# Head pairs of an RWKV layer: three levels of a triangular inverse as a loop on TensorE, and two products moved to GpSimd

## The reference

```python
def wkv_scan(r, decay, k, v, a_vec, b_vec, s0, reverse):
    def step(s, inp):
        r_t, w_t, k_t, v_t, a_t, b_t = inp
        sa = jnp.einsum('bhvk,bhk->bhv', s, a_t)
        s = s * w_t[:, :, None, :] + sa[..., None] * b_t[:, :, None, :] + v_t[..., None] * k_t[:, :, None, :]
        return s, jnp.einsum('bhvk,bhk->bhv', s, r_t)
    xs = tuple(jnp.swapaxes(t, 0, 1) for t in (r, decay, k, v, a_vec, b_vec))
    s_final, ys = lax.scan(step, s0, xs, reverse=reverse)
    return jnp.swapaxes(ys, 0, 1), s_final
...
for d in range(N_DIRS):
    yc_d, s_ctx = wkv_scan(r_c, dec_c, k_c, vh_c, -kk_c, kk_c * a_c, s0, reverse)
    yx_d, _ = wkv_scan(r_x, dec_x, k_x, vh_x, -kk_x, kk_x * a_x, s_ctx, reverse)
```

## Time and profile before

| | us |
|---|---|
| median of three runs | 4356.76 |
| lowest and highest | 4350.53, 4363.58 |
| the profiled execution | 4341.01 |
| its span from first to last instruction | 4339.2 |
| mean granted TensorE clock | 0.963 |

### The profile page before, as it was taken

The page is one execution under the profiler, slowest core; times in us unless marked ns, Lnnn a source line. Parts: engine busy times, 40 slices in busy tenths (PEclk is TensorE's granted clock), DMA queues, the critical chain, the costliest instruction groups (busy, mean ns, idle before and its releaser), DMA issues.

```text
span 4339.2 us, 93368 instructions
## 1 busy us (share of the span) xinstructions
PE 3897.5 (90%) x39960; PEld 2507.8 (58%) x39960; DVE 1669.7 (38%) x3445; ACT 852.2 (20%) x1847; POOL 663.0 (15%) x643
## 2 busy tenths in 40 slices
PE   5989999989967777777889998999999989999998
PEld 4534444445456766766444444447688854658887
DVE  2512122154545445445232112453345424515363
ACT  2200000020154444444100001115000011330000
POOL 4100000000022222222000000000334310003343
PEclk8989999999989999999899999999999999999999
DMA  8387887851200000000369996110122221102221
GB/s 334 142 307 293 333 333 293 335 218 72 81 8 13 13 13 13 13 13 17 136 264 428 429 429 277 59 59 1 65 91 78 78 86 39 40 20 78 93 82 39
DMA packets 54242, 619.74 MB, mean 143 GB/s; under 512 B 5648, under 2 KB 8976, under 8 KB 18320
## 3 DMA queue, kind: packets, MB, share of 16 engines
q1 hardware_dynamic: 49664, 599.41, 35.0%
q10 hardware_dynamic: 2448, 9.05, 0.6%
q0 software_dynamic: 1792, 6.29, 0.5%
HBM read 602.40 MB, written 12.32 MB: 142 GB/s over the span
## 4 chain that ended last, share of the span: by engine, by line
issue 44%; PE 42%; DMA 4%; DVE 3%; POOLq 3%; POOL 2%; ACT 1%; DVEq 0%; PEld 0%; SPq 0%; ACTq 0%; PEldq 0%
PE bank L891 29%; PE bank L1362 12%; DMA ring<-slabs 3%; POOL work L3257 1%; POOLq L3260 1%; POOLq L3258 1%; DMA kv<-work 1%; POOLq L3174 1%; POOL work L3261 1%; PE bank L1409 1%; DVE work L2699 0%; DVE work L2379 0%; PEld bank L891 0%; ACT work L2084 0%; DVE work L2723 0%
## 5 line engine op out<-in xcount | busy, mean ns | idle before, releaser
L891 PE MATMUL bank<-ring,work 128*32 128x256 f32 (+3 forms) x7002 | 765.6, 440 | 71.0 <-DMA ring<-slabs 59.1
L891 PE MATMUL bank<-work 128*128 128x256 f32 (+8 forms) x3590 | 785.8, 430 | 26.1 <-DVE work L3100 15.9
L891 PEld LDWEIGHTS bank<-work 128*128 128x128 f32 (+3 forms) x3590 | 500.5, 184 | 298.2 <-issue 212.7
L891 PEld LDWEIGHTS bank<-ring,work 128*32 128x32 f32 (+2 forms) x7002 | 317.9, 124 | 493.5 <-issue 387.2
L891 PE MATMUL bank<-work,ring 128*128 128x256 f32 (+1 forms) x1616 | 480.7, 456 | 12.1 <-DVE work L3119 5.1
L891 PE MATMUL bank<-hx,ring 128*128 128x512 f32 (+1 forms) x1344 | 482.8, 515 | 6.6 <-DVE hx L2394 4.5
L1362 PE MATMUL bank<-work 64*64 64x64 f32 x11520 | 338.5, 233 | 123.8 <-issue 87.2
L891 PEld LDWEIGHTS bank<-work,ring 128*128 128x128 f32 x1616 | 306.6, 191 | 181.2 <-issue 134.2
L1362 PEld LDWEIGHTS bank<-work 64*64 64x64 f32 x11520 | 309.6, 144 | 162.0 <-issue 158.1
L891 PEld LDWEIGHTS bank<-hx,ring 128*128 128x128 f32 x1344 | 256.7, 192 | 220.5 <-issue 200.2
L3177 POOL TENSOR_TENSOR work<-work 128x512 f32<-128x512 f32 (+1 forms) x30 | 34.4, 1156 | 1458.1 <-ACT work L1913 1458.1
(11 more groups left out here) (317 smaller groups left out, 4587.2 us busy)
## 6 DMA issues: line engine op xcount, KB each, us to landing
ring<-slabs SPq DMA_DIRECT2D x228, 2048.0 KB, 10.0
work<-slabs SPq DMA_DIRECT2D x48, 2048.0 KB, 18.3
work<-kv SPq DMA_DIRECT2D x18, 384.0 KB, 3.2
kv<-work SPq DMA_DIRECT2D x2, 3072.0 KB, 15.7
kv<-work ACTq DMA_DIRECT2D x6, 512.0 KB, 17.6
work<-tabs ACTq DMA_DIRECT2D x1, 2176.0 KB, 8.2
resx<-xT SPq DMA_DIRECT2D x1, 2048.0 KB, 10.9
outT<-hx ACTq DMA_DIRECT2D x8, 256.0 KB, 2.1
```

Source lines behind the costliest of these rows:

```text
L891: return pe.matmul(out, lhsT, rhs, start=(k == 0), stop=(k == n - 1))
```

## The change

Levels 2, 3 and 4 become a loop of three turns on TensorE alone; the other engines stay written out. A loop's waits need numbers that grow by the same amount each turn, so the steps of levels leave the common orders and get semaphores of their own: `lv_dve` for T additions, `lv_act` for copies, `lv_pool` for masks, with orders `LV_DVE`, `LV_ACT` and `LV_POOL`. The chain steps leave levels 2 to 4: four (d = 0) or five (d = 1) come between the values' products, three stay in level 1, four (d = 0) or three (d = 1) stand in level 5. Gate and bonus products come after level 5. The sums of the key norm, the variance and the gate use other banks. `decayed_bs` and `decayed_keys` run on GpSimd, after the masks of level 4 and of level 5. The core of the diff:

```diff
+LV_DVE, LV_ACT, LV_POOL = [], [], []
+EARLY = (4, 5)
...
+    RK_PE += [("x0", _d, 0), ("pre", _a, 0), ("pre", _a, 1), ("x0", _d, 1), ("x0", _d, 2)] + _zs(1)
+    RK_PE += [("mv", _d, 0)] + _zs(1) + [("mv", _d, 1)] + _zs(1) + [("mv", _d, 2)] + _zs(1)
+    RK_PE += [("kn", 0)] * _d + _zs(_d) + [("kn", 1), ("var",)] * _d
     for _l in range(1, 6):
...
+        _n = _l in (1, 5)
+        RK_PE += [("T", _d, _l, 0), ("T", _d, _l, 1)] + _zs(_n) + [("T", _d, _l, 2), ("XX", _d, _l, 0)] + _zs(_n)
+        RK_PE += [("XX", _d, _l, 1)] + _zs(_l == 5) + [("XX", _d, _l, 2)] + _zs(_n)
+    RK_PE += [("gate",), ("bonus",)] * _d
...
-RK_BANK = {"vt": (0, 1), "x0": (2, 3, 2), "mv": (0, 1, 0), "kn": (4, 5), "var": (7,), "T": (2, 3, 2), "gate": (7,), "bonus": (6,), "mean": (6,),
+RK_BANK = {"vt": (0, 1), "x0": (2, 3, 2), "mv": (0, 1, 0), "kn": (1, 4), "var": (5,), "T": (2, 3, 2), "gate": (5,), "bonus": (6,), "mean": (6,),
...
+            def level_products(d, l, b):
+
+                out = P[RK_BANK["T"][b]]
                 for q, c in enumerate(chunks(b)):
                     m = heads2(out[:, q * CH:(q + 1) * CH], NL[:, c, :], X[:, c, :], across=l > 1)
-                m.then_inc(rk_pe, rk.one("T", d, l, b))
+                return m
...
+            def middle_levels(p, d):
+
+                nl, xx, ts = (lv_count(order, p, (name, d, 2, 0)) for order, name in ((LV_POOL, "nl"), (LV_ACT, "XX"), (LV_DVE, "T")))
+                with pe.Fori(0, 3) as i:
+                    for b in range(3):
+                        pe.wait_ge(lv_pool, i * 3 + (nl + b))
+                        pe.wait_ge(lv_act, i * 3 + (xx - 3 + b))
+                        if b == 2:
+                            pe.wait_ge(lv_dve, i * 3 + ts)
+                        pe.sem_inc(pe_steps)
+                        level_products(d, 2, b).then_inc(rk_pe, 1)
+                    for b in range(3):
+                        pe.wait_ge(lv_dve, i * 3 + (ts + b))
+                        if b == 2:
+                            pe.wait_ge(lv_act, i * 3 + xx)
+                        pe.sem_inc(pe_steps)
+                        double_products(d, 2, b).then_inc(rk_pe, 1)
...
             def scores(p, d, b):
...
-                outb, = banks(p, "sb", d, b, after=[("dve", 0, "kds", d)])
+                outb, = banks(p, "sb", d, b, after=[("pool", 0, "kds", d), ("dve", 0, "arr", d)])
...
                     first_levels(p, d, 1, 2)
-                    values_in(p, d)
+                    chain(p, a, 1)
+                    values_in(p, d, 0)
+                    chain(p, a, 2)
+                    values_in(p, d, 1)
+                    chain(p, a, 3)
+                    values_in(p, d, 2)
+                    chain(p, a, 4)
                     if d == 1:
-                        key_sums(p)
+                        key_sums(p, 0)
+                        chain(p, a, 5)
+                        key_sums(p, 1)
                         head_sums(p, "var", sqs, "act", ("sq",))
...
+                    j = EARLY[d]
+                    level_t(p, d, 1, 0)
+                    level_t(p, d, 1, 1)
+                    chain(p, a, j + 1)
+                    level_t(p, d, 1, 2)
+                    level_x(p, d, 1, 0)
+                    chain(p, a, j + 2)
+                    level_x(p, d, 1, 1)
+                    level_x(p, d, 1, 2)
+                    chain(p, a, j + 3)
+                    middle_levels(p, d)
+                    level_t(p, d, 5, 0)
+                    level_t(p, d, 5, 1)
+                    chain(p, a, j + 4)
+                    level_t(p, d, 5, 2)
+                    level_x(p, d, 5, 0)
+                    chain(p, a, j + 5)
+                    level_x(p, d, 5, 1)
+                    chain(p, a, j + 6)
+                    level_x(p, d, 5, 2)
+                    if d == 0:
+                        chain(p, a, j + 7)
+                    else:
+                        gate_product(p)
+                        head_sums(p, "bonus", ksr, "dve", ("ksr",))
...
-                act.wait_ge(*(rk_done("dve", p, "pp") if d == 0 else rk_done("dve", p - 1, "kds", 0)))
+                act.wait_ge(*(rk_done("dve", p, "pp") if d == 0 else rk_done("pool", p - 1, "kds", 0)))
...
-            def decayed_bs(p, d):
-
-                v.wait_ge(*rk_done("dve", p, "ksm", d))
-                v.tensor_tensor(bd, bd, E3, ALU.mult).then_inc(rk_dve, rk.next("bds", d))
...
+            def decayed_bs(p, d):
+
+                pool.wait_ge(*rk_done("dve", p, "ksm", d))
+                pool.wait_ge(*rk_done("act", p, "exps", d))
+                pool.tensor_tensor(bd, bd, E3, ALU.mult).then_inc(rk_pool, rk.next("bds", d))
+
+            def decayed_keys(p, d):
+
+                pool.tensor_tensor(kd, kd, E3, ALU.mult).then_inc(rk_pool, rk.next("kds", d))
...
+                        if l == 4:
+                            decayed_bs(p, 1 - d)
+                        elif l == 5:
+                            decayed_keys(p, 1 - d)
```

More of the change, by code:

```diff
@@ L161 @@
         _by = {"sb": ("act", ("nt",) + _rest), "sk": ("dve", ("mt",) + _rest), "mean": ("dve", ("cen",)), "gate": ("dve", ("res",))}
[L162 removed]
+        _by.update({_q: ("dve", _name) for _q in ("x0", "ar", "bonus")}, T=("lvd", _name))
         RK_READ[_name] = {RK_BANK[_k][_rest[-1] if _rest else 0]: [_by.get(_k, ("act", _name))]}
@@ L1372, in banks @@
                 freed = [(engine, before) + step for steps in RK_FREE[name].values() for engine, step, before in steps
-                         if not (front and (step[0] in ("bonus", "res", "XX") or engine == "act" and step in RK_ACT[:RK_ACT.index(("pw", 0))])) and not (back and step[0] != "z")]
+                         if not (front and (step[0] in ("bonus", "res", "mv") or engine == "act" and step in RK_ACT[:RK_ACT.index(("pw", 0))])) and not (back and step[0] != "z")]
                 for engine in ("dve", "act", "pool"):
@@ L1378, in banks @@
                         pe.wait_ge(*rk_done(engine, p + last[0], *order[last[1] - 1]))
+                for engine, order in (("lvd", LV_DVE), ("lva", LV_ACT), ("lvp", LV_POOL)):
+                    last = max(((-step[1], place_in(order, step[2:])) for step in list(after) + freed if step[0] == engine), default=None)
+                    if last and p + last[0] >= 0:
+                        pe.wait_ge(*lv_done(engine, p + last[0], *order[last[1] - 1]))
                 pe.sem_inc(pe_steps)
@@ L1388, in first_levels @@
                 for b in groups:
-                    out, = banks(p, "x0", d, b, after=[("pool", 0, "nl", d, 0, b)])
+                    out, = banks(p, "x0", d, b, after=[("lvp", 0, "nl", d, 0, b)])
                     for q, c in enumerate(chunks(b)):
@@ L1486, in inverse_times @@
             def inverse_times(p, d, b):
-                out, = banks(p, "wu", d, b, after=[("act", 0, "XX", d, 5, b), ("act", 0, "mv", d, b)])
+                out, = banks(p, "wu", d, b, after=[("lva", 0, "XX", d, 5, b), ("act", 0, "mv", d, b)])
                 for q, c in enumerate(chunks(b)):
@@ L2853, in _ @@
                     first_levels(p, d)
-                    steps = iter(range(1, NCH))
+                    for j in range(1, EARLY[d] + 1):
+                        chain(p, a, j)
+                    steps = iter(range(EARLY[d] + 1, NCH))
                     for l in range(1, 6):
@@ L2857, in _ @@
                         level(p, d, l, 1)
-                        for j in itertools.islice(steps, 1):
-                            chain(p, a, j)
+                        if l in (1, 5):
+                            chain(p, a, next(steps))
                         level(p, d, l, 2)
-                        for j in itertools.islice(steps, 1):
-                            chain(p, a, j)
+                        if l in (1, 5):
+                            chain(p, a, next(steps))
                         if l == 1:
@@ L2868, in _ @@
                             decayed_sums(p, a)
-                        elif l == 4:
-                            decayed_bs(p, a)
-                        for j in itertools.islice(steps, 1):
-                            chain(p, a, j)
+                        if l in (1, 5):
+                            chain(p, a, next(steps))
+                        if l == 5 and d == 0:
+                            chain(p, a, next(steps))
                         if l == 1 and d == 1:
```

112 lines of the change are left out of this document (51 added, 61 removed).

## The result

| | before | after |
|---|---|---|
| median (runs) | 4354.55 us (4) | 4320.44 us (4) |
| lowest and highest | 4350.53, 4363.58 | 4310.69, 4327.15 |
| the profiled execution | 4341.01 | 4327.15 |
| the stage, first addition of x0 (cut 0.2 us ahead of it) to last state copy | 1223.1 to 2075.1, 852.0 | 1238.7 to 2058.8, 820.1 |

The ratio is 0.9917, 95% interval 0.9894 to 0.9939: faster by 34 us. Forecast was 4334 (23 us less), with 4312 to 4344 for the likeliest case alone. The stage of the profiles doesn't hang on that. The stage got 31.9 us shorter where the sum said 24.

A forecast was written before the change was run, and what follows sets the result against it. TensorE, standing for its own code packets, was taken as the bound; loop, chain steps, decays and the rest summed to -1.4 us even, -1.6 odd, -23 in all, giving 4334 us; range leaving out two in ten 4292 to 4375.

The forecast's parts named there:

- the likeliest case: Whole kernel: the change takes it to 4334 us, own range 4312 to 4344; chance 0.45 for -13 to -45 us.
- the sum: Pass over the head pairs: -1.4 us an even and -1.6 an odd half-pass, eight pairs -24, with the prologue -23.
- The bound: Pass over the head pairs: TensorE's code comes one packet at a time, 4 us each; it stands about 1 us a packet.
- The loop: Levels 2 to 4 on TensorE: 14.5 us as a loop, saving 3.2 us an even and 3.0 an odd half-pass.
- The chain steps: Early part, levels 1 and 5: moved steps make TensorE work and stand there, +2.6 us even, +1.7 odd half-pass.
- The decays: Inverse-decay products moved from VectorE to GpSimd: -0.5 us an even half-pass, 0 odd, +1 before the loop over p.
- More comes back: Half-passes: chain's waits hide in code waits, a level takes 3.9 us; about -4 us a half-pass, 4293 us; chance 0.13.
- A wash: Levels 2 to 4: a level takes 4.9 us and the chain takes the saving; 4344 to 4370 us; chance 0.20.
- the two slower ones for chain and GpSimd: Moved steps stand 0.54 us each: 4387 us, chance 0.15; level 5's masks late by 1.8 us: 4363 to 4375, 0.04.
- Branches that fetch: TensorE's loop: each taken branch takes 3.86 us, 124 us in all; about 4458 us; chance 0.03.

The follow-up runs named there:

- the small kernels: Two kernels of their own: 1728 plain matmuls, written out or looped 101.0 us each; matmuls in the level's order (64 columns), 96.8 us written out, 71.2 us looped.

## Why the prediction was right

**The bound.** Right, and now shown: 128 matmuls and a stop. Code came at 3.45 to 4.01 us a packet where I read 4.0 to 4.5, and a packet holds 256 records, not 249. In the small kernels the price of a packet is that time less the time TensorE needs for it, so nothing at 29.2 ns a matmul and about 1 us at 20.6.

**The loop.** 145 packets (140 to 150 forecast), "issue" -46 us (-25 to -50), branches of 212 ns, levels 2 to 4 in 14.0 and 13.1 us (14.5). The term was mis-sized: a level takes 3.83 us, not 4.2, so that 3.7 and 4.4 us a half-pass (without gate and bonus) were saved, for 3.2 and 3.0. Not all of it is the loop's: with the loop undone levels 2 to 4 take 15.4 and 15.1 us, so 2.3 and 2.4 us of it come from what left these levels. What the term left out is the gain behind the loop: with the loop undone, "rest" is 1.1 to 1.8 us longer, where the forecast had 0.3. That the fetch gets ahead during the loop would explain it; it fits the 0.8 to 1.0 us of "issue" there, but no row shows it.

**The chain steps.** The place was right, the form not. In the early part I expected waits of 1 to 2 us; the profile shows one of 0.4 a half-pass, and the part is still 1.4 and 1.2 us longer (1.9 and 1.4 were put there), since a step and the values' product beside it follow at the chain's pace of some 0.8 us. The waits forecast for level 5 don't exist in the profile: no row of the chain's update there. Together with what their absence saves in levels 2 to 4, chain steps, banks and decays lose 19 us of stage where there is no loop to gain by them.

**The decays.** 2.27 and 1.81 us on GpSimd for 1.8 twice; the masks of level 5 end no wait of TensorE. The forecast -0.5 a pair was read from one half-pass; in the trace of before that wait is 1.1 us once, 0.2 to 0.3 three times and absent in the other four even half-passes. So without the loop the move gained nothing. With it the move hides 0.7 us in both halves of a pair, but the 4.4 us of stage are less than the profiles tell: that they are -0.5 a pair is luck as far as is shown. Ahead of the loop over p it cost 1.4 us (waits of 10.5 for 9.1), for 1.

**The sum.** 8 x (-3.7 - 4.4 + 3.0 + 1.1) = -32 in the stage, where 3.0 and 1.1 are the growth of all other parts in the table (odd: less the 2.1 that only moved). Against the forecast's -24 the levels gave 15 us more and the other parts cost 7 more. The experiments cut it another way: the loop gave 51 us where 8 x (3.2 + 3.0 + 0.3 + 0.3) = 54 was booked, and chain steps and decays cost 19 where 8 x (2.6 + 1.7 - 0.5) = 30 was. That the loop's total came so near is partly luck, since half of it was saved elsewhere than forecast. From the clock in the earlier trace rows I had charged 0.6 us a stretch and did not see that shorter waits also bring less of it: 75.1 us at 1.2 GHz fell to 47.8.

**The rivals.** "More comes back" had the level (3.9) right and the chain too cheap. "A wash" and the two slower ones for chain and GpSimd fall with the rows above. "Branches that fetch" is real, but for bodies of 2304 records and more, not of 288 or 1360.

## What to carry to other kernels

Where TensorE runs small matmuls written out, look at the instruction queue: if packets of code stand as far apart as the stops, try a loop whose body is kept; here it gave 51 us of stage, more than any reordering tried, and the reordering made for the loop's sake lost 19 by itself. Then look at what ends the longest single waits, because half of those of over 2 us were paid again in clock here; and look again afterwards, because a stop for code can take the place of a wait. And keep VectorE's SBUF work away from GpSimd's long instructions, or it goes at one instruction for one.

## What the runs showed of the hardware that was not expected

- Code for TensorE comes at 3.45 to 4.01 us a packet of 256 records, with nothing else on the queues; loops of 288, 600 and 1360 records are kept, one of 2304 is fetched anew in each turn and stands about 6 us at the branch.
- VectorE's SBUF instructions beside GpSimd's run one for one: 0.42 becomes 2.02 (one source), 0.68 becomes 2.28 (two), 0.28 becomes 4.6 beside a 128x2048 instruction; reading PSUM, 0.41 stays 0.41. Which engine pays differs: in the stage GpSimd's masks went from 0.64 to 1.29 beside products of VectorE that kept their 0.95.
- Matmuls of 8 columns back to back ran at a granted clock of 0.51 for 120 us, nearly all at 1.2 GHz, though TensorE's rows show no idle time.
